# Two output projections run token tile 0 two units ahead, and the normalizations behind them start on tile 0 while the projection is still running

## The chip, the cores and the metric

The kernel runs on one core of one Trainium2 chip. The metric is the device time of one execution in microseconds (us), the median over several runs. The engines are called TensorE (PE, matmuls; its weight loads are PEld), VectorE (DVE), ScalarE (ACT), GpSimd (POOL) and SyncE (SP, which issues most transfers).

## The reference, cut to what matters

The program is two model blocks in a row on 1024 tokens of width 1024. The second block has an even and an odd layer; the even layer also carries 256 context tokens. What the change touches is the end of the even layer, the begin of the odd one and the very end:

```python
# even layer, tokens x and context xc alike
x_new = x + gt * _even_mix(_pre(x, e_norm[i], sh, sc), *args)      # ends in concat(y_a, y_b) @ w_out
xc = xc + gt_c * _even_mix(_pre(xc, e_norm[i], sh_c, sc_c), *args)
# odd layer
cb, cc, cx, cg, q, k, v, ag = _odd_proj(_pre(x, o_norm[i], sh, sc), o_w_in[i])
att = _window_attention(_apply_rope(q, cos, sin), _apply_rope(k, cos, sin), v, k_c, v_c, o_sink[i])
x_new = x + gt * _odd_out(cb, cc, cx, cg, att, ag, o_c_conv_w[i], o_w_out[i])
# end
return _rmsnorm(x, final_norm)
# _pre(x, g, shift, scale) = _rmsnorm(x, g) * (1 + scale) + shift
```

## The kernel before, in words

Activations lie transposed: 128 features on the partitions, 8 chunks of features, tokens along the free dimension. Tokens are cut into tile 0 (tokens 0 to 511), tile 1 (512 to 1023) and, where the context takes part, tile 2 (256 columns); `TILES2` is all three, `TILES1` the first two. A weight *unit* is 128 output features by 1024 input features. A *job* is one unit on one tile: 8 steps k, one for each chunk of input features, and each step is three matmuls (`mm3`: high x high, low x high, high x low), so that float32 accuracy comes out of a faster number format. Every weight and every activation is therefore split into a high part (a cast on ScalarE, `split_hi`, L163) and a low part (a subtraction on VectorE, `split_lo`, L168). Three units fit in the weight buffers, and `units_begun` lets SyncE load the unit after next.

The order on each engine is written out by hand, stage after stage; engines meet at counting semaphores. The stages concerned, in order:

- `eout`: the even output projection, 8 units x 3 tiles, unit by unit (`linear`). After each job VectorE adds the gated product to the residual (L2264), ScalarE squares the result (L230), VectorE adds the square to a running sum (L235). The last job is (unit 7, tile 2).
- `norm5`: the root mean square norm in front of the odd layer. For each tile: 4 small matmuls against the constant `inv_d` (each two instructions, `pe_cols`, L397) give the mean of squares in columns; ScalarE takes the root (L358), VectorE the reciprocal (L439) and four diagonal tiles (L442); a matmul with `ones` (two instructions, `pe_spread`, L402) spreads the factor over a bank. Then for each of 8 chunks VectorE makes the normed value (L466), ScalarE shifts it and writes the high part (L386, L389), and the low part is made on VectorE (even chunks, L427) or on GpSimd (odd chunks, L429). In the kernel before all of this stands behind the last job of `eout`.
- `oin`: the odd input projection. Its first two units, k and v, run as a pair (`first_pair`): tile 0 of both interleaved, then k on tiles 1 and 2, the rest of v. Units for q and the gate follow. A unit's raw weights are loaded once `norm5` is ready.
- `win`: windowed attention, with the convolution branch filled into it; it ends with four products `ycH`, `ycL` (L2500, L2543).
- `oout`: the odd output projection, 8 units x 2 tiles, unit by unit. It reads `ycH/ycL` for steps 0 to 3 and the attention output `qH/qL` for steps 4 to 7. Residual (L2615), square, sum as in `eout`; ScalarE also multiplies by the final gain in place (L2629).
- `norm6`: the final norm: both tiles' `pe_cols`, roots, `pe_spread`, a copy of the factor (L362), and 16 multiplications of 128x512 by that factor, 11 on VectorE (L457) and 5 on GpSimd (L416). SyncE stores each chunk as it gets ready (L2599).

Two helpers that the kernel has already and uses elsewhere: `run_jobs` takes a list of jobs (unit, tile), runs a few of them interleaved at first (`paired`, each `trail` steps behind the one before), calls `between(pe, j, k)` ahead of step k of job j, and waits for a bank where `need(j)` says so. `lagged(units, tiles)` makes such a list in which tile 0 of a unit stands ahead of the other tiles of the unit before:

```python
def lagged(units, tiles, begin=1):
    jobs = [(v, 0) for v in range(begin)]
    for v in range(begin, units):
        jobs += [(v, 0)] + [(v - begin, ti) for ti in range(1, tiles)]
    return jobs + [(v, ti) for v in range(units - begin, units) for ti in range(1, tiles)]
```

Of the kernel before, what the change touches and what calls it, by code (L numbers as in the profile page):

```python
# [24 lines left out]
ALU = mybir.AluOpType  # L25
# [5 lines left out]
P = 128  # L31
D = 1024
KC = D // P
# [66 lines left out]
def build(nc, t):  # L100
# [13 lines left out]
    with es:  # L114
# [123 lines left out]
        class Norm:  # L238
# [36 lines left out]
            def pool_low(self, j):  # L275

                return bool(self.outs) and j % 2 == 1 or self.scaled and j % 3 == 2
# [1482 lines left out]
        def mod_norm(name, layer, tmp, x_ready, squares=None):  # L1760
            return Norm(name, lambda c, ti: tile_of(x, c, ti), TILES2,
                        lambda c, ti: gmod[:, layer, c, vec(ti):vec(ti) + 1],
                        lambda c, ti: modv[:, 24 * layer + c, vec(ti):vec(ti) + 1],
                        lambda part, c, ti: tile_of(u2L if part else u2H, c, ti), tmp, sum_banks=(6, 7, 5), x_ready=x_ready,
                        squares=squares, sum_order=None if squares else [2, 0, 1])


# [466 lines left out]
        eout_squares = Squares("eout_squares", TILES2, A_B)  # L2234
# [5 lines left out]

        def eout_act(act):
            def square(i, s):
                for ti, (c0, n) in enumerate(TILES2):
                    j = (2 * i + s) * T3 + ti
                    act.wait_ge(eout_drained, j + 1 + 2 * T3)
                    f = bass.ds(2 * i + s, 1)
                    src = (hx[:, f, c0:c0 + n] if ti < 2 else x[1][:, f, :]).rearrange("p a n -> p (a n)")
                    eout_squares.act(act, j, (s * T3 + ti) % 2, src, n)

            for v in range(8):  # L2250
                square(v // 2, v % 2)
                split_hi(act, W0["eout"] + v + 2)

        def eout_dve(dve):
            eout_squares.start(dve)
            dve.wait_ge(landed, 80 + 32)
            for i in range(0, 4):
                for s in range(2):
                    for ti, (c0, n) in enumerate(TILES2):
                        dve.wait_ge(eout_done, (2 * i + s) * T3 + ti + 1)  # L2260
                        f = bass.ds(2 * i + s, 1)
# [559 lines left out]
```

## Time and profile before

| what | value |
|---|---|
| time, median of 3 runs | 2137.5 us (2136.45 to 2140.7) |
| profiled execution: time, span of its instructions | 2136.24 us, 2134.4 us |
| TensorE busy, mean granted clock | 96% of the span, 0.985 of full speed |
| VectorE, ScalarE, GpSimd busy | 61%, 36%, 11% |
| TensorE from the last matmul of `eout` to the end of the k and v units | 1567.8 to 1610.7 us |
| `oout` from its first matmul to its last | 2021.0 to 2109.8 us |
| from the last matmul of `oout` to the end | 24.5 us |

The span runs from the first to the last instruction; the time has launch and end around it. Times in the text are counted from the start of the span. The granted clock is a share of 2.4 GHz; it has two levels, 1.0 (2.4 GHz) and 0.5 (1.2 GHz). A busy share says little about what a stage is worth: what counts is which wait ends last in it.

### The profile page before, as it was taken

The page shows a single profiled execution, that of the slowest core. Times are in us where ns is not written, and L with a number is a line of the kernel's source. Part 1 is how long each engine was busy: PE and PEld are TensorE (multiplying, and loading weights), DVE is VectorE, ACT ScalarE, POOL GpSimd, SP SyncE. Part 2 cuts the span into 40 slices and gives each one's busy share as a digit, 9 for nine tenths or more (in the row PEclk, how much of TensorE's full clock was granted, in tenths as well). Part 3 has the DMA queues.
Part 4 walks back from the last instruction along what each step waited for, and adds up shares of the span by engine and source line. Part 5 has one row for each costly group of instructions (what it writes and reads, how often), then busy time and mean ns, then how long its engine had stood idle before and what let it go on. Part 6 is the DMA issues. An engine that isn't in the chain of part 4 may idle for free. (4 is left out here: it accounts for less than half of the span.)

```text
span 2134.4 us, 25901 instructions
## 1 busy us (share of the span) xinstructions
PE 2046.6 (96%) x10182; PEld 1685.3 (79%) x10182; DVE 1298.7 (61%) x2236; ACT 768.7 (36%) x1433; POOL 238.1 (11%) x211
## 2 busy tenths in 40 slices
PE   6999999999999999999999999989999999999796
PEld 4877887888888888887788888778877877888685
DVE  7378867742652562464589896774363356776634
ACT  4256544311310220223441242642152335555432
POOL 2032313000000000002310010000020012222101
PEclk9999999999999999999999999999999999999997
DMA  3102001411321321331231056133122211111212
GB/s 135 60 21 99 31 22 64 162 59 54 131 75 48 109 109 50 109 109 40 65 124 37 34 142 161 67 111 151 40 93 69 79 45 38 38 38 37 105 49 79
DMA packets 47736, 164.75 MB, mean 77 GB/s; under 512 B 5632, under 2 KB 10368, under 8 KB 46464
## 3 DMA queue, kind: packets, MB, share of 16 engines
q1 hardware_dynamic: 43584, 147.02, 20.1%
q0 software_dynamic: 1584, 7.29, 1.7%
q10 hardware_dynamic: 2448, 8.79, 1.1%
q8 instruction: 81, 1.33, 0.2%
q14 instruction: 39, 0.32, 0.1%
HBM read 135.86 MB, written 19.93 MB: 73 GB/s over the span
## 5 line engine op out<-in xcount | busy, mean ns | idle before, releaser
L173 PE MATMUL banks<-u2H,wH 128*128 128x512 f32 (+1 forms) x912 | 347.7, 381 | 11.2 <-POOL u2L L429 6.1
L174 PE MATMUL banks<-u2L,wH 128*128 128x512 f32 (+1 forms) x912 | 338.8, 371 | 0.0
L175 PE MATMUL banks<-u2H,wL 128*128 128x512 f32 (+1 forms) x912 | 338.5, 371 | 0.0
L163 ACT CAST wH<-raw 128x1024 fp32r<-128x1024 f32 x153 | 160.0, 1047 | 288.4 <-DMA raw<-in_wstream 286.4
L173 PE MATMUL banks<-aH,wH 128*128 128x512 f32 x640 | 252.3, 394 | 1.9 <-DVE wL L168 1.7
L175 PE MATMUL banks<-aH,wL 128*128 128x512 f32 x640 | 249.3, 389 | 0.0
L174 PE MATMUL banks<-aL,wH 128*128 128x512 f32 x640 | 249.2, 389 | 0.0
L168 DVE TENSOR_TENSOR wL<-raw,wH 128x1024 fp32r<-128x1024 f32 x153 | 189.4, 1239 | 85.6 <-ACT wH L163 85.2
L173 PEld LDWEIGHTS banks<-u2H,wH 128*128 128x128 f32 x912 | 173.1, 190 | 46.3 <-issue 11.3
L173 PE MATMUL banks<-mH,wH 128*128 128x512 f32 x512 | 200.6, 392 | 2.1 <-DVE wL L168 1.1
L175 PE MATMUL banks<-mH,wL 128*128 128x512 f32 x512 | 199.9, 391 | 0.0
L174 PE MATMUL banks<-mL,wH 128*128 128x512 f32 x512 | 199.9, 390 | 0.0
L175 PEld LDWEIGHTS banks<-u2H,wL 128*128 128x128 f32 x912 | 172.8, 189 | 30.0
L174 PEld LDWEIGHTS banks<-u2L,wH 128*128 128x128 f32 x912 | 173.2, 190 | 28.6 <-issue 1.4
L1942 DVE SCALAR_TENSOR_TENSOR conv_out<-conv_in,par,conv_out 128x1295 f32<-128x1295 f32 x108 | 162.7, 1565 | 0.6
L1100 POOL TENSOR_SCALAR logits<-logits,stat 128x256 f32<-128x256 f32 (+3 forms) x96 | 121.4, 1278 | 340.7 <-DVE stat L975 340.7
L173 PEld LDWEIGHTS banks<-aH,wH 128*128 128x128 f32 x640 | 120.2, 188 | 27.7 <-DVE wL L168 2.2
L175 PEld LDWEIGHTS banks<-aH,wL 128*128 128x128 f32 x640 | 120.2, 188 | 25.1
L174 PEld LDWEIGHTS banks<-aL,wH 128*128 128x128 f32 x640 | 120.3, 188 | 24.5 <-issue 0.5
L1649 DVE TENSOR_TENSOR hm<-banks,hm 128x512 f32<-128x512 f32 x48 | 32.9, 691 | 173.5 <-PE banks L175 173.5
L1508 ACT ACTIVATE relu<-banks 128x512 f32<-128x512 f32 x64 | 38.2, 598 | 244.3 <-PE banks L175 244.3
L1613 DVE SCALAR_TENSOR_TENSOR mod_junk<-mod_w,cvec 128x1024 bf16<-128x1024 f32 x96 | 117.5, 1224 | 5.0
(311 smaller groups left out, 3693.4 us busy)
## 6 DMA issues: line engine op xcount, KB each, us to landing
raw<-in_wstream SPq DMA_DIRECT2D x153, 512.0 KB, 3.5
mod_w<-in_mod_w SPq DMA_DIRECT2D x48, 512.0 KB, 5.2
side_sum<-side_tap POOLq DMA_DIRECT2D x11, 647.5 KB, 5.8
gt<-gates_scratch SPq DMA_DIRECT2D x8, 640.0 KB, 3.9
h<-in_x SPq DMA_DIRECT2D x4, 1024.0 KB, 10.8
hm<-in_x SPq DMA_DIRECT2D x1, 4096.0 KB, 12.3
x_scratch<-x_out SPq DMA_DIRECT2D x2, 2048.0 KB, 7.4
hx<-x_scratch SPq DMA_DIRECT2D x1, 4096.0 KB, 12.2
```

The lines of the kernel that those rows point to most:

```text
L163: act.copy(wH[:, u % R, :], raw[:, u % R, :]).then_inc(weights_hi, 1)
L168: eng.tensor_tensor(wL[:, u % R, :], raw[:, u % R, :], wH[:, u % R, :].bitcast(F32), ALU.subtract)\
L173: first = pe.matmul(out, aH, bH, start=start, stop=False)
L174: pe.matmul(out, aH, bL, start=False, stop=False)
L175: return first, pe.matmul(out, aL, bH, start=False, stop=stop)
L1100: m = pool.tensor_scalar(src, src, stat[:, SUM, k % 3, hs:hs + 1], None, ALU.mult)
L1508: act.activation(relu[:, j % 2, :], bank(j % 4), ACT.Relu).then_inc(up_drained, 1)
L1613: dve.scalar_tensor_tensor(mod_junk[:], mod_w[:, m, :], 1.0, cvec[:, v, :], ALU.mult, ALU.mult, accum_out=modv[:, n, v:v + 1]).then_inc(mo ...
L1649: dve.tensor_tensor(dst, bank(4 + s * 2 + ti), dst, ALU.add).then_inc(down_drained, 1)
L1942: dve.scalar_tensor_tensor(dst, src, w, dst, ALU.mult, ALU.add).then_inc(conv_step, 1)
```

## The change: what it does

1. `eout` goes through a list in which tile 0 of unit v runs ahead of tiles 1 and 2 of unit v-1. The last tile-0 job is thus number 19 of 0 to 23, and four jobs, (6,1), (6,2), (7,1), (7,2), follow it. Into them the norm of tile 0 is put: `pe_cols` ahead of step 4 and `pe_spread` ahead of step 7 of job 20 on TensorE, and root, values, high and low parts of 8 chunks written out in order between the remaining residuals, squares and sums on ScalarE, VectorE and GpSimd. The first two splits of `oin`'s weights stand in the same order. A square root of a constant ahead of the square of job 19 has ScalarE load the table early.
2. Since `y` is still read then, tile 0 of the normed activations gets another place (`w2H`, `w2L`), q moves to where it was, and so do the buffers of the squares and of the values and, in `oout`, `xo`.
3. `oin`'s k and v run as (0,0) and (1,0), interleaved with the second two steps behind, then (0,1), (1,1), (0,2), (1,2). `pe_cols` of tiles 1 and 2 stand ahead of steps 2 and 3 of the first job, `pe_spread` ahead of steps 5 and 6. ScalarE and VectorE take the norm of tiles 1 and 2 there, and take k and v out of the banks in the new order.
4. `oout` runs its list in the same lagged order. Steps 4 to 7 (attention) of jobs (0,0) and (1,0) stand first and wait for the attention of tile 0 only; then steps 0 to 3 of both, which wait for `ycL`. The norm of tile 0 stands in jobs 14 and 15; its 8 final multiplications stand between the residuals of jobs 14 and 15. GpSimd has no part in the final norm any more, VectorE makes all 16 multiplications. Here too a square root of a constant loads the table early.

The core of the diff:

```diff
+        EOUT = [(0, 0)] + [job for v in range(1, 8) for job in ((v, 0), (v - 1, 1), (v - 1, 2))] + [(7, 1), (7, 2)]
+        def eout_split(j):
+            return {0: 2, 4: 3, 7: 4, 10: 5, 13: 6, 16: 7}.get(j)
         def eout_act(act):
+            for j in range(19):
+                eout_square(act, j)
+                if eout_split(j):
+                    split_hi(act, W0["eout"] + eout_split(j))
+            act.activation(rms_cols[:, 2, 0:1], eps[:, 0:1], ACT.Sqrt)
+            eout_square(act, 19)
+            split_hi(act, W0["oin"])
+            norm5.act_root(act, 0)
+            eout_square(act, 20)
+            norm5.act_high(act, 0)
+            norm5.act_high(act, 1)
+            eout_square(act, 21)
+            for c in range(2, 5):
+                norm5.act_high(act, c)
+            split_hi(act, W0["oin"] + 1)
+            norm5.act_high(act, 5)
+            eout_square(act, 22)
+            norm5.act_high(act, 6)
+            norm5.act_high(act, 7)
+            eout_square(act, 23)
         def eout_dve(dve):
+            for j in range(20):
+                eout_residual(dve, j)
+                eout_add(dve, j)
+                if eout_split(j):
+                    split_lo(dve, W0["eout"] + eout_split(j))
+            split_lo(dve, W0["oin"])
+            norm5.dve_root(dve, 0)
+            eout_residual(dve, 20)
+            eout_add(dve, 20)
+            norm5.dve_value(dve, 0)
+            norm5.dve_value(dve, 1)
+            norm5.dve_low(dve, 0)
+            eout_residual(dve, 21)
+            eout_add(dve, 21)
+            norm5.dve_value(dve, 2)
+            norm5.dve_value(dve, 3)
+            norm5.dve_low(dve, 2)
+            norm5.dve_value(dve, 4)
+            norm5.dve_value(dve, 5)
+            norm5.dve_low(dve, 4)
+            split_lo(dve, W0["oin"] + 1)
+            eout_residual(dve, 22)
+            norm5.dve_value(dve, 6)
+            eout_add(dve, 22)
+            norm5.dve_value(dve, 7)
+            norm5.dve_low(dve, 6)
+            eout_residual(dve, 23)
+            eout_add(dve, 23)
         def eout_pe(pe):
-            linear(pe, W0["eout"], 8, TILES2, hl2(yH, yL), eout_done, eout_drained)
+            def between(pe, j, k):
+                if (j, k) == (20, 4):
+                    norm5.pe_cols(pe, 0, 20)
+                if (j, k) == (20, 7):
+                    norm5.pe_spread(pe, 0)
+            run_jobs(pe, W0["eout"], EOUT, TILES2, hl2(yH, yL), lambda j: EOUT[j][0] % 2 * T3 + EOUT[j][1], eout_done, eout_drained,
+                     None, 0, between, need=eout_need)
+        w2H = [sb("w2H0", [KC, TN], A_B, F32R), *u2H[1:]]
+        w2L = [sb("w2L0", [KC, TN], A_B + 16 * KB, F32R), *u2L[1:]]
+        OIN_KV = [(0, 0), (1, 0), (0, 1), (1, 1), (0, 2), (1, 2)]
         def oin_pe(pe):
-            norm5.pe(pe)
-            first_pair(pe, O0, TILES2, hl2(u2H, u2L), lambda s, ti: s * T3 + ti, S["kv_done"], norm5)
+            def between(pe, j, k):
+                if (j, k) in ((0, 2), (0, 3)):
+                    norm5.pe_cols(pe, k - 1, 24)
+                if (j, k) in ((0, 5), (0, 6)):
+                    norm5.pe_spread(pe, k - 4)
+            run_jobs(pe, O0, OIN_KV, TILES2, hl2(w2H, w2L), lambda j: OIN_KV[j][0] * T3 + OIN_KV[j][1], S["kv_done"], S["k_drained"],
+                     norm5, 2, between, need=lambda j: 0, trail=2)
...
+        OOUT = lagged(8, 2)
+        def oout_split(j):
+            return {0: 2, 3: 3, 5: 4, 7: 5, 9: 6, 11: 7}.get(j)
+        def oout_scale(dve, ti):
+            norm6.wait(dve, "rstd_ready", ti + 1)
+            dve.wait_ge(xo_scaled, 14 + 2 * ti)
+            for c in range(KC):
+                dve.tensor_tensor(norm6.x(c, ti), norm6.x(c, ti), norm6.rs[:, ti, :], ALU.mult).then_inc(norm_sems["ready"], 1)
-        def oout_pool(pool):
-            pool.wait_ge(xo_scaled, 2 * KC)
-            norm6.pool(pool)
         def oout_dve(dve):
+            for j in range(14):
+                residual(j)
+                if oout_split(j):
+                    split_lo(dve, W0["oout"] + oout_split(j))
+            norm6.dve_root(dve, 0)
+            residual(14)
+            oout_scale(dve, 0)
+            residual(15)
+            norm6.dve_root(dve, 1)
+            oout_scale(dve, 1)
         def oout_act(act):
+            for j in range(13):
+                square(j)
+                gain(j)
+                if oout_split(j):
+                    split_hi(act, W0["oout"] + oout_split(j))
+            act.activation(rms_cols[:, 2, 0:1], eps[:, 0:1], ACT.Sqrt)
+            square(13)
+            gain(13)
+            norm6.act_root(act, 0)
+            factor(0)
+            for j in (14, 15):
+                square(j)
+                gain(j)
+            norm6.act_root(act, 1)
+            factor(1)
         def oout_pe(pe):
-            pe.wait_ge(S["yc_lo"], HALF)
-            pe.wait_ge(win_o_lo, 2 * NB)
+            blocks = [(0, OQ, False), (1, OQ, False), (0, OY, True), (1, OY, True)] + [(j, OQ + OY, True) for j in range(2, 16)]
+            pe.wait_ge(S["cg_drained"], 2 * HALF)
+            pe.wait_ge(win_o_lo, NB)
+            for n, (j, ks, ends) in enumerate(blocks):
+                if n == 2:
+                    pe.wait_ge(S["yc_lo"], HALF)
+                if n == 4:
+                    pe.wait_ge(win_o_lo, 2 * NB)
+                for i, k in enumerate(ks):
+                    if (j, i) == (14, 4):
+                        norm6.pe_cols(pe, 0, 14)
+                    if (j, i) == (15, 0):
+                        norm6.pe_spread(pe, 0)
...
+            norm6.pe_cols(pe, 1, 16)
+            norm6.pe_spread(pe, 1)
```

## Rows read from the trace of the kernel before

**Rows 1.** Chain that ended last, its end: start us, length us, what.

```profile
2109.87 0.76 DVE xo L2615
...
2112.07 2.74 PE banks L397 x16
2114.81 2.00 PE banks L402 x2
```

**Rows 2.** Timeline of TensorE, end of `eout` to q: start, length, [idle before].

```profile
1567.53 0.28 PE L175 MATMUL banks<-yHc,wL 128*128 128x256 f32 x1
1569.29 3.54 PE L397 MATMUL banks<-inv_d,eout_squares_acc 128*128 128x1 f32 x20 [1.49 <-DVE eout_squares_acc L235]
...
1577.22 0.47 PE L173 MATMUL banks<-u2H,wH 128*128 128x512 f32 x1
...
1613.41 0.50 PE L173 MATMUL banks<-u2H,wH 128*128 128x512 f32 x1 [2.67 <-DVE wL L168]
```

**Rows 3.** Timeline of TensorE, end of `win` and first jobs of `oout`.

```profile
2013.11 0.28 PE L894 MATMUL banks<-pT2L,vz2L 128*128 128x256 f32 x1
2020.99 0.77 PE L173 MATMUL banks<-ycH,wH 128*128 128x512 f32 x1 [7.60 <-PEq L195]
...
2028.07 0.39 PE L173 MATMUL banks<-ycH,wH 128*128 128x512 f32 x1
```

**Rows 4.** Timeline of TensorE at 34 us: a norm inside a running stream.

```profile
34.85 1.05 PE L339 MATMUL banks<-inv_d,x_squares_acc 128*128 128x1 f32 x8 [0.52 <-DVE x_squares_acc L235]
35.77 0.48 PE L173 MATMUL banks<-uH,wH 128*128 128x512 f32 x1
...
37.38 1.13 PE L346 MATMUL banks<-norm_sq,ones 128*128 128x512 f32 x2
```

**Rows 5.** Groups by line, 1456 to 1570 us: busy us, mean ns | idle before.

```profile
L2264 DVE SCALAR_TENSOR_TENSOR hx<-banks,modv,hx 128x512 f32<-128x512 f32 x16 | 12.0, 750 | 48.1 <-PE banks L175 36.4 <-DMA xc<-in_ctx 11.7
L235 DVE TENSOR_TENSOR eout_squares_acc<-eout_squares_acc,eout_squares_sq 128x512 f32<-128x512 f32 x16 | 11.1, 692 | 11.2 <-ACT eout_squares_sq L230 11.2
L230 ACT ACTIVATE eout_squares_sq<-hx 128x512 f32<-128x512 f32 x16 | 10.1, 634 | 77.2 <-DVE hx L2264 77.2
L168 DVE TENSOR_TENSOR wL<-raw,wH 128x1024 fp32r<-128x1024 f32 x8 | 9.8, 1226 | 4.1 <-ACT wH L163 4.1
```

**Rows 6.** Groups by line, 1574 to 1601 us, the chunks of `norm5`.

```profile
L466 DVE SCALAR_TENSOR_TENSOR norm_v<-hx,gmod,banks 128x512 f32<-128x512 f32 x16 | 11.2, 737 | 0.8 <-PE banks L402 0.8
L429 POOL TENSOR_TENSOR u2L<-norm_v,u2H 128x512 fp32r<-128x512 f32 x8 | 10.4, 1296 | 272.2 <-ACT u2H L389 272.2
...
L427 DVE SCALAR_TENSOR_TENSOR u2L<-norm_v,modv,u2H 128x512 fp32r<-128x512 f32 x8 | 7.0, 878 | 1.1
```

**Rows 7.** Line L235 over the run: duration ns min/median/max, first and last start.

```profile
L235 DVE TENSOR_TENSOR x_squares_acc<-x_squares_acc,x_squares_sq x16: 676/692/1604, 7.5 to 33.2; 128x512 f32<-128x512 f32 x16
```

**Rows 8.** Windows: us, busy of PE, PEld, DVE, ACT, POOL; clock; DMA.

```profile
1570.00:1573.00 3.00, 3.00 (x17) 3.00 (x17) 2.85 (x11) 1.67 (x4) 0.00 (x0) 0.55 1.20 513
...
2008.00:2011.00 3.00, 2.12 (x16) 1.91 (x16) 3.00 (x4) 1.35 (x4) 0.00 (x0) 1.00 0.83 360
...
2021.00:2024.00 3.00, 3.00 (x7) 2.42 (x8) 1.30 (x1) 0.00 (x0) 0.00 (x0) 0.50 0.27 83
```

**Rows 9.** Timeline of ScalarE at the begin of the kernel.

```profile
3.28 1.28 ACT L623 ACT_TABLE_LOAD   x1 [3.28 <-issue]
```

**Rows 10.** Page, part 6: transfers, KB each, median us to landing.

```profile
raw<-in_wstream SPq DMA_DIRECT2D x153, 512.0 KB, 3.5
```

**Rows 11.** Timeline of VectorE in the final norm.

```profile
2119.74 3.41 DVE L457 TENSOR_TENSOR xo<-xo,norm_rs 128x512 f32<-128x512 f32 x2
...
2126.40 1.88 DVE L457 TENSOR_TENSOR xo<-xo,norm_rs 128x512 f32<-128x512 f32 x3
...
2128.81 0.68 DVE L457 TENSOR_TENSOR xo<-xo,norm_rs 128x512 f32<-128x512 f32 x1
```

**Rows 12.** Timeline of the SP queue: the last store.

```profile
2131.05 0.61 SPq L2599 DMA_DIRECT2D out_y<-xo  x1
```

More of the change, by code:

```diff
@@ L2239, in eout_sp, with eout_square @@
             loads(sp, "eout", "eout")
-        def eout_act(act):
[L2242 to L2252, printed above, removed]
+        def eout_square(act, j):
+            act.wait_ge(eout_drained, j + 1)
+            eout_squares.act(act, j, j % 2, eout_x(j), TILES2[EOUT[j][1]][1])
@@ L2338, in oin_act @@
         def oin_act(act):
-            norm5.act(act)
+            norm5.act_root(act, 1)
+            norm5.act_root(act, 2)
+            for j in range(KC, 3 * KC):
+                norm5.act_high(act, j)
             norm5.wait_ready(act, 3 * KC)
@@ L2387, in oin_dve @@
             dve.memset(zeros[:], 0.0)
-            norm5.dve(dve)
+            for ti in (1, 2):
+                norm5.dve_root(dve, ti)
+            for j in range(KC, 3 * KC):
+                norm5.dve_value(dve, j)
+                if j > KC:
+                    norm5.dve_low(dve, j - 1)
+            norm5.dve_low(dve, 3 * KC - 1)
             dve.wait_ge(S["rope_loaded"], 32)
@@ L2637, in oout_pe, with residual @@
-        def oout_pe(pe):
-            pe.wait_ge(S["yc_lo"], HALF)
-            pe.wait_ge(win_o_lo, 2 * NB)
-            linear(pe, W0["oout"], 8, TILES1,
-                   lambda part, k, c0, n: ((ycL if part else ycH)[:, k, c0:c0 + n] if k < HALF else
-                                           (qL if part else qH)[:, k - HALF, c0:c0 + n]), oout_done, oout_drained)
-            norm6.pe(pe)
+            def residual(j):
+                dve.wait_ge(oout_done, j + 1)
+                dve.scalar_tensor_tensor(oout_x(j), bank(oout_bank(j)), modv[:, 40 + OOUT[j][0], 0:1], oout_x(j), ALU.mult, ALU.add)\
+                    .then_inc(oout_drained, 1)
+                oout_squares.dve(dve, j, j % 2, OOUT[j][1], TN)
@@ new lines, in oout_dve, with square, gain, factor @@
+            for j in range(14):
[8 more added lines that the diff above has]
+            oout_scale(dve, 1)
+        def oout_act(act):
+            def square(j):
+                act.wait_ge(oout_drained, j + 1)
+                oout_squares.act(act, j, j % 2, oout_x(j), TN)
+            def gain(j):
+                act.activation(oout_x(j), oout_x(j), ACT.Copy, scale=pcol("final_norm2", OOUT[j][0])).then_inc(xo_scaled, 1)
+            def factor(ti):
+                norm6.wait(act, "spread", ti + 1)
+                act.copy(norm6.rs[:, ti, :], bank(norm6.sum_banks[ti])).then_inc(norm_sems["rstd_ready"], 1)
+            for j in range(13):
[13 more added lines that the diff above has]
+            factor(1)
```

113 lines of the change are left out of this document (58 added, 55 removed).

## The prediction, made before the change was run

> **What bounds the kernel now.** I read the chain that ended last first. It runs through TensorE almost everywhere, so only time in which TensorE waits, or works at half clock, can be won, plus what follows its last job. The end of the chain shows the second: job 15 of `oout` is over when its residual starts at 2109.87, and then come residual, square, sum, small matmuls, spread, copy and multiplications one after the other, with TensorE at the slow end of its speed (16 instructions of L397 in 2.74 us, 2.00 us for one spread) [rows 1]. The span ends at 2134.4, 24.5 us after the last job.
>
> The timeline of TensorE shows the first. `eout` ends at 1567.8 (1567.53 + 0.28); the k and v units end at 1613.41 - 2.67 = 1610.7 [rows 2]. That is 42.9 us for work of 2 units. An ordinary 512-column job takes (2109.87 - 2028.07) / 15 = 5.45 us [rows 1, 3], 0.68 a step; a 256-column job I put at 2.9, a little over half. Two units are 2 x (5.45 + 5.45 + 2.9) = 27.6 us, so 15.3 us there are norm and waits: small matmuls and spreads fill 1569.3 to 1577.2, at clock 0.55 in the window shown [rows 2, 8]. The third place is the begin of `oout`: TensorE is idle for 7.60 us, from 2013.4 to 2020.99, and then works at clock 0.50 [rows 3, 8]: the first job takes 7.08 us instead of 5.45, 1.63 lost.
>
> **Part 1: the norm of tile 0 inside `eout`, k and v on tile 0 first.** Call t the end of job 19, the last on tile 0. Jobs 20 to 23 hold 5.45 + 2.9 + 5.45 + 2.9 = 16.7 us, so in the kernel before `eout` ends at t + 16.7 and k and v at t + 59.6.
>
> In the new kernel: residual 0.75, square 0.63, sum 0.69 [rows 5] end at t + 2.2; `pe_cols` stands at step 4 of job 20, t + 2.7, and doesn't wait. In a running stream eight of these instructions push the next matmul back by 0.92 us (35.77 - 34.85), a spread takes 1.13 [rows 4]. Root, reciprocal and diagonals have three steps, 2.0 us, until the spread; the whole norm of three tiles took 7.9 us [rows 2], 2.6 a tile, so at worst 0.6 is missing; I take 0. `eout` thus ends 2.05 later, at t + 18.7, and tile 0's factor is there at t + 6.8.
>
> VectorE sets the rest. Its list makes it wait for job 20 (t + 7.5) ahead of the first value; residual, square, sum bring it to t + 9.7. Then without a break, by [rows 5, 6], the 256-column forms at 0.6 of the others: 8 values (5.9), 4 low parts (3.5), one weight split (1.2), residuals and sums of jobs 21 to 23 (1.65 and 1.5): 13.8 us, so the last sum ends at t + 23.5 with no wait for ScalarE. I add 0.8 for ScalarE, whose squares and high parts stand between, and 0.5 for GpSimd: a sum that meets GpSimd took up to 1.604 instead of 0.692 [rows 7], three sums at most 2.7. That gives t + 24.8.
>
> TensorE has done two steps of k by t + 20.0 and stands at `pe_cols` of tile 1 until t + 24.8: a new stall of 4.8 us, behind which everything of `oin` is queued. Then 0.92 + two steps + 0.5 + four steps, and the spread of tile 1: t + 31.5. Tile 1's chunks follow at 2 x 0.74 + 0.88 a pair [rows 6], 9.4 for four pairs, and 1.7 for the last high part and GpSimd's low part (1.30): t + 42.6. TensorE, done with the tile-0 pair at t + 37.5, ends (0,1) at t + 43.4 and has 5.45 + 2.9 + 2.9 left: t + 54.7. So 4.9 us are won at full clock. What was 42.9 us from `eout`'s end becomes 36.0, but `eout` ends 2.0 later.
>
> The clock takes some back. A stall of 7.60 us was followed by 1.63 lost; the three `pe_cols` of before ran at half clock, 3.54 us for 20 instructions [rows 2] against 2.3 at the price of [rows 4]. I take both here: 1.63, and 0.75 for two of the three tiles, 2.4 in all, so **2.5 us won**; the bounds are 4.9 (the clock holds) and 0 (GpSimd's 2.2 us more on top). The window at 2008 speaks for the first: TensorE was idle for 0.88 of 3.00 us and the clock stayed 1.00; the one at 1570, behind an idle time of only 1.49, speaks for the second [rows 2, 8].
>
> The Trainium skill (TensorE: Matmul & The Clock Gate, Why this matters for your kernels) says that a long idle gap between bursts of matmuls in mid-kernel puts the engine back to half its rate. By that rule the new stall is paid for and the sum stays at 2.5; by the window at 2008 alone it would be 4.9.
>
> The stall of 2.67 us behind v [rows 2] stays: the last copy of v and the two splits of q's first weights still follow the last job. Those weights are loaded when the norm is ready, at about t + 48, some 6.7 us before they are wanted, and a unit lands in 3.5 [rows 10]; the rope table goes ahead of it in the same queue. Every us past that cover would cost one.
>
> At nothing I put: the lagged order in `eout` (unit 2 is wanted after four jobs and not six, but its split hangs on job 0's residual; later units have three jobs between load and use, 13.8 us against 3.5 for the transfer [rows 10] and about 4 for residual, square and both splits, the cast estimated at twice a square for its 1024 columns [rows 5]); the early loads of ScalarE's table (1.28 us [rows 9], while it waits for a job of 5.45; if not covered, or reloaded by the squares, 1.3 each); the moved buffers; the spill of `hx`, issued behind the last residual as before, with nothing waiting for it soon.
>
> **Part 2: `oout`.** The first two blocks are 8 steps, 5.45 us, and start at 2013.4, where TensorE was idle; they end at 2018.85. The wait for `ycL` ends as before, near 2020.9. Ahead of the end of job 13 there are then 14 x 5.45 - 5.45 = 70.8 us: 2091.7, or 2091.5 with the first matmul's own latency out. Before, the second but last job ended its predecessor at 2109.85 - 10.9 = 2098.95: 7.4 won, 5.45 by the early blocks, the rest by the clock, which I let hold over a gap of 2 us; lower bound 5.8.
>
> Behind job 13: 5.45 + 0.92 + 1.13 + 5.45 = 12.95 to the end of job 15. VectorE waits in the sum of job 14 for ScalarE, which is held by the copy of the factor (spread at 7.5; copy, like a square, to 8.2; square): 9.4. Its 8 multiplications: four starts lie 2.41 apart without GpSimd (2126.40 to 2128.81), 0.60 each, against 3.41 for a pair beside GpSimd [rows 11]. They end at 14.2, so residual 15 starts 1.3 late; sum at 16.3. TensorE has been idle for 3.4 us, and I take the prices of [rows 1]: half of 2.74, root and diagonals 1.5, spread 2.00, copy 0.63: the first product is ready at 23.0, the last near 27.2. From the stores: seven issues of 0.61 and the 3.35 us from the last issue (2131.05) to the end [rows 12] give 30.6. From the products: the last one of before ended at 2129.49 [rows 11], 4.9 us ahead of the end, which gives 32.1. Between them I take 31.4. Before, the same stretch was 2134.4 - 2098.95 = 35.45. **4.0 won**; at full clock 5.8. The end is 2091.5 + 31.4 = 2122.9, **11.5 won** in this part, bounds 8 and 13.3.
>
> **The sum.** 2.5 + 11.5 = 14.0 us off the profiled execution's 2136.24: 2122.2. The median of the runs lies 1.26 above that execution, so I forecast 2123.5 for the median.
>
> **The rivals.**
> *A. VectorE and GpSimd get in each other's way in the norm.* For it: the maximum of [rows 7]; against it: the median there is 0.692 and the low parts, 0.878 in the mean, hold the meetings already. Three sums and a split at 0.9 more are 3.1 beyond my 0.5: the sum of job 23 at about t + 27.9, part 1 at -0.6, time 2126.6. From t + 27.3 on the part wins nothing. The Trainium skill (GPSIMD Engine Reference, Key points) says that GpSimd shares its SBUF interfaces with VectorE and contends with instructions that read two SBUF inputs, which the sums and splits do; [rows 11] agree, 3.41 us for two products beside GpSimd against 1.88 for three alone, and by that rule it is this time that comes out.
> *B. The clock holds* at the stall in `oin` and at the end: 4.9 + 13.3 = 18.2, time 2119.3. For it the window at 2008 [rows 8], against it the other two.
> *C. Late weights in the last projection make it slower.* Unit v + 3 is loaded when tile 1 of unit v has ended and split behind the job that starts then: residual 0.75, square 0.63, gain and cast some 1.9 (three times a square, an estimate), split 1.23 [rows 5], 4.5 of the 5.45 us that the next job gives. A load that lands more than 8.5 us after its issue holds TensorE up in each of five units; 2.8 us in each, from a landing of 11.3, eat up all 14.0, and at 12 us the time is 2141. Against it: 3.5 us in the median of 153 [rows 10].
> *D. The change does not do what it says:* the splits and hand-written lists only move the waits, and all that is won is the 5.45 of the early blocks: 2132. For it the 13.8 us of VectorE's unbroken work; against it that TensorE's own waits, 15.3 and 7.6 us, lie at the very places.
>
> **Chances and range.** Forecast 0.5, A 0.24, B 0.2, C 0.02, D 0.04. From B's time less a little to A's with the bounds of part 2 (8 - 0.6: 2130.1) I give 2118 to 2129. A measurement of this kernel tells 0.2%, 4.3 us, from no change. Faster by more 0.95, within 0.03, slower 0.02.
>
> **What would show it.** The new profile should show: `eout` ending 2 us later, and in job 20 no wait at L397 or L402; a stall of about 4.8 us at L397 behind two steps of k, ended by VectorE's sum, and clock 0.5 behind it; k and v ending some 2 to 3 us earlier; the 2.67 us ahead of q unchanged; `oout`'s first matmul at 2013 on this scale, a gap of 2 us, no wait for weights; 12 to 13 us from job 13 to 15, 18 from there to the end. I am wrong if VectorE's sum of job 23 is much later than t + 25, if q's weights come late, or if weights are waited for in the lagged order.

## The result, and the profile after

The changed kernel takes 2126.0 us in the median of four runs, the kernel before 2139.1 beside it: ratio 0.9945 [0.9931, 0.9958], 13 us faster by the medians and 11.8 by the ratio; a second set gave 0.9945 [0.9933, 0.9957]. The profiled execution took 2123.12 us, its span is 2121.3, TensorE is busy for 96% of it at a mean clock of 0.991. The forecast was 2123.5, the range 2118 to 2129. The total came out 2.5 us above the forecast; of the two parts that make it up, the first gave nothing and the second what was forecast or a little more.

Part 1 first. The timeline of TensorE in the changed kernel, from `eout`'s end (1569.51) to q; this answers [rows 2]:

```profile
1570.52 0.39 PE L175 MATMUL banks<-w2H,wL 128*128 128x512 f32 x1
1576.49 1.87 PE L339 MATMUL banks<-inv_d,eout_squares_acc 128*128 128x1 f32 x8 [5.59 <-DVE eout_squares_acc L235]
...
1580.92 0.85 PE L339 MATMUL banks<-inv_d,eout_squares_acc 128*128 128x1 f32 x4
...
1585.57 1.02 PE L346 MATMUL banks<-norm_sq,ones 128*128 128x512 f32 x2
...
1609.67 0.28 PE L175 MATMUL banks<-u2H,wL 128*128 128x256 f32 x1
...
1613.18 0.50 PE L173 MATMUL banks<-w2H,wH 128*128 128x512 f32 x1 [3.23 <-DVE wL L168]
```

After two steps of k TensorE stands for 5.59 us until VectorE's last sum, as foretold, and then works slowly: the eight small matmuls take 1.87 us, against 1.05 for eight such in [rows 4]. The windows of the same kernel show the clock behind the stall (the columns are those of [rows 8]):

```profile
1573.00:1577.00 4.00, 0.51 (x3) 0.51 (x3) 3.01 (x5) 1.66 (x3) 1.26 (x1) 0.59 0.62 262
1577.00:1581.00 4.00, 4.00 (x15) 3.42 (x14) 1.05 (x5) 0.26 (x1) 0.00 (x0) 0.50 0.91 393
1581.00:1585.00 4.00, 4.00 (x15) 3.34 (x14) 0.65 (x3) 0.26 (x1) 0.00 (x0) 0.63 1.03 389
1585.00:1589.00 4.00, 4.00 (x18) 2.96 (x17) 2.24 (x4) 1.56 (x3) 0.00 (x0) 1.00 0.15 57
```

The half clock falls on the very instructions that the next stretch of the norm waits for. Why the sum itself is late is seen in the same kernel's timeline of VectorE, which shows two of its three last sums:

```profile
1563.57 1.31 DVE L235 TENSOR_TENSOR eout_squares_acc<-eout_squares_acc,eout_squares_sq 128x256 f32<-128x256 f32 x1 [0.48 <-ACT eout_squares_sq L230]
...
1575.15 1.28 DVE L235 TENSOR_TENSOR eout_squares_acc<-eout_squares_acc,eout_squares_sq 128x256 f32<-128x256 f32 x1 [0.70 <-ACT eout_squares_sq L230]
```

and in that of GpSimd at the same times:

```profile
1563.31 1.28 POOL L429 TENSOR_TENSOR w2L<-norm_v,w2H 128x512 fp32r<-128x512 f32 x1 [250.67 <-ACT w2H L308]
...
1574.89 1.26 POOL L429 TENSOR_TENSOR w2L<-norm_v,w2H 128x512 fp32r<-128x512 f32 x1 [2.82 <-ACT w2H L308]
```

Each sum of 256 columns begins while a low part of GpSimd runs, and ends 0.29 and 0.28 us behind it; in the kernel before, such a sum took 0.42 to 0.43 us. The Trainium skill (SBUF — State Buffer, SBUF: two separate sides) says that whichever of the two engines starts first holds the shared port pair for its whole instruction when VectorE reads two SBUF inputs; these four rows agree, except that the sums end less than 0.42 us behind GpSimd, so not all of a sum waited.

Part 2: the timeline of TensorE at the begin and at the end of `oout`, which answers [rows 1, 3]:

```profile
2013.53 0.40 PE L173 MATMUL banks<-qH,wH 128*128 128x512 f32 x1
...
2021.07 0.50 PE L173 MATMUL banks<-ycH,wH 128*128 128x512 f32 x1 [1.91 <-DVE ycL L2624]
...
2108.14 1.05 PE L339 MATMUL banks<-inv_d,oout_squares_acc 128*128 128x1 f32 x8 [3.34 <-DVE oout_squares_acc L235]
2110.67 2.07 PE L346 MATMUL banks<-norm_sq,ones 128*128 128x512 f32 x2 [1.48 <-DVE norm_sq L317]
```

and of VectorE at the end, with the last residual and the 8 multiplications of tile 1:

```profile
2105.95 0.74 DVE L2711 SCALAR_TENSOR_TENSOR xo<-banks,modv,xo 128x512 f32<-128x512 f32 x1
...
2113.39 4.90 DVE L2695 TENSOR_TENSOR xo<-xo,norm_rs 128x512 f32<-128x512 f32 x8 [2.78 <-ACT norm_rs L2736]
```

The first blocks start where TensorE idled before, and a wait of 1.91 us is left of 7.60. The last residual starts at 2105.95, the last product ends at 2118.29. From the end of the attention on TensorE (in the changed kernel the start of the first block, 2013.5) to the end of the span it is 2121.3 - 2013.5 = 107.8 us, against 2134.4 - 2013.4 = 121.0: 13.2 won in this execution.

### The profile page after: what moved, and what is told of

Its sections match the earlier page's. It is cut to its first block and busy times, and to the rows that moved or that the text cites. A ratio compares the mean times of both kernels' runs of the same rounds, so it can differ in the third digit from the quotient of the medians.

```text
span 2121.3 us, 25905 instructions
## 1 busy us (share of the span) xinstructions
PE 2038.9 (96%) x10182; PEld 1679.8 (79%) x10182; DVE 1298.2 (61%) x2241; ACT 767.6 (36%) x1435; POOL 229.4 (11%) x206
## 3 DMA queue, kind: packets, MB, share of 16 engines
q0 software_dynamic: 1584, 7.29, 1.8%
## 5 line engine op out<-in xcount | busy, mean ns | idle before, releaser
L173 PE MATMUL banks<-u2H,wH 128*128 128x512 f32 (+1 forms) x704 | 260.0, 369 | 3.9 <-POOL u2L L429 2.1
L174 PE MATMUL banks<-u2L,wH 128*128 128x512 f32 (+1 forms) x704 | 256.3, 364 | 0.0
L175 PE MATMUL banks<-u2H,wL 128*128 128x512 f32 (+1 forms) x704 | 256.3, 364 | 0.0
L173 PEld LDWEIGHTS banks<-u2H,wH 128*128 128x128 f32 x704 | 133.3, 189 | 26.7 <-issue 3.7
L175 PEld LDWEIGHTS banks<-u2H,wL 128*128 128x128 f32 x704 | 133.1, 189 | 21.3
L174 PEld LDWEIGHTS banks<-u2L,wH 128*128 128x128 f32 x704 | 133.4, 190 | 20.1 <-issue 0.2
## 6 DMA issues: line engine op xcount, KB each, us to landing
hm<-in_x SPq DMA_DIRECT2D x1, 4096.0 KB, 13.6
hx<-x_scratch SPq DMA_DIRECT2D x1, 4096.0 KB, 12.1
```

The costliest lines, as they stand in the source:

```text
L173: first = pe.matmul(out, aH, bH, start=start, stop=False)
L174: pe.matmul(out, aH, bL, start=False, stop=False)
L175: return first, pe.matmul(out, aL, bH, start=False, stop=stop)
```

## The experiments

All ratios are to the kernel before, run on the same chip. Distances "behind `eout`" are counted from the end of its last matmul: in the changed kernel the last sum is at 6.9, the end of tile 1's spread at 17.1, the end of k and v at 40.4, the start of q at 43.7; in the kernel before, k and v end at 42.9 and q starts at 45.6, but `eout` is some 1.8 us shorter there. In the twelve profiled executions with the changed `eout` its end lies anywhere from 1569.5 to 1573.7 us, so rows of different executions are compared within a stage and not by their place in the span.

### The parts by themselves

```diff
part1_only: eout_*, oin_* of after; oout_*, norm6 of before
part2_only: eout_*, oin_* of before; oout_*, norm6 of after
```

> The even output projection and the odd input projection of the changed kernel, with the last projection and the final norm of the kernel before. Theory T: the chain from the last sum to the spread of tile 1 ran at half clock and ate what the early norm of tile 0 gained, so k and v end where they did and this part alone is worth 0 to 0.5 us of 2139 (ratio 0.9998, between 0.9995 and 1.0005). The prediction's sum: 2.5 us won, ratio 0.9988. Rival: the part loses by itself (late weights of q, a longer eout) and only looks neutral beside part 2: ratio above 1.001.

> The even output projection and the odd input projection of the kernel before, with the last projection and the final norm of the changed kernel. Theory T: all of the gain is here, 13.4 us from the end of the attention to the end of the span: ratio 0.9937, time about 2126. By the prediction's sizes 11.5 us: 0.9946. Rival: part 1 gives part of it (its buffers or its earlier k and v help later stages): under 10 us, ratio above 0.9953.

Part 1 alone: 2138.5 us, ratio 1.0001 [0.9992, 1.001]. Part 2 alone: 2126.0 us, 0.9944 [0.9931, 0.9956]. The gain is all in part 2, and the prediction's 2.5 us for part 1 (0.9988) lie outside the interval. Part 2's 12.0 us by the ratio agree with 11.5 as well as with 13.2.

### The clock behind the stall

```diff
+                if (j, k) == (0, 2):
+                    for i in range(23):
+                        pe.matmul(bank(3), wH[:, O0 % R, 0:P], w2H[0][:, 0, :], start=True, stop=True)
                 if (j, k) in ((0, 2), (0, 3)):
                     norm5.pe_cols(pe, k - 1, 24)
```

> The changed kernel with 23 additional matmuls of 128x512 (operands that are there already, into a bank that is not in use and is opened anew later) ahead of the small matmuls of tile 1, in the stall of 5.59 us; they compute nothing that is read. Theory T, the clock ate the gain: with TensorE busy the granted clock stays at 1.00 behind the stall, the 8 small instructions take 0.9 us instead of 1.87, the spread of tile 1 ends 6.7 us behind the last sum instead of 10.2, and k and v end 3.4 us earlier: time 3.4 us under the changed kernel, ratio to the kernel before 0.9929. Rival 1, the clock falls whatever TensorE does there: no difference, 0.9945. Rival 2, the later waits (chunks of tile 1, weights of q) take it back: spread 3.4 us earlier, but q starts less than 1 us earlier, ratio 0.994 to 0.9945.

Ratio 0.9926 [0.9914, 0.9939], 4 us under the changed kernel; the two intervals overlap, so the rows have to carry the reading. TensorE's timeline of this kernel, with the stall filled:

```profile
1578.38 1.05 PE L339 MATMUL banks<-inv_d,eout_squares_acc 128*128 128x1 f32 x8 [0.42 <-DVE eout_squares_acc L235]
...
1583.94 1.02 PE L346 MATMUL banks<-norm_sq,ones 128*128 128x512 f32 x2
```

and its windows:

```profile
1577.00:1581.00 4.00, 3.58 (x22) 2.82 (x21) 2.63 (x7) 0.27 (x1) 1.04 (x1) 1.00 1.23 524
1581.00:1585.00 4.00, 4.00 (x18) 3.02 (x18) 0.66 (x4) 0.26 (x1) 0.00 (x0) 1.00 0.91 393
```

The sum comes at the same distance (7.0), but the spread ends at 13.6 instead of 17.1 and k and v at 37.0 instead of 40.4: 3.4 us, as theory T had it, and q starts 4.0 us earlier, so that rival 2 falls. Work that computes nothing pays here, because the clock stays at 1.00 for the chain behind it.

### The place of the wait

```diff
-                if (j, k) in ((0, 2), (0, 3)):
-                    norm5.pe_cols(pe, k - 1, 24)
-                if (j, k) in ((0, 5), (0, 6)):
+                if (j, k) in ((0, 6), (1, 4)):
+                    norm5.pe_cols(pe, 1 + j, 24)
+                if (j, k) in ((1, 5), (1, 6)):
                     norm5.pe_spread(pe, k - 4)
```

> The changed kernel with the small matmuls of tiles 1 and 2 moved back in the pair on tile 0: ahead of steps (0,6) and (1,4), the spreads ahead of (1,5) and (1,6). Ten steps of tile 0 (6.8 us) then stand where TensorE idled for 5.59 us. Theory T, the place of the wait cost the stall and the clock: no stall over 0.5 us, clock 1.00, spread of tile 1 done some 11.4 us after eout's end instead of 17.2, last chunk of tile 1 about 22.6 us after it instead of 28.3, k and v end 5 to 6 us earlier; q waits for its weights some 3.5 us as before: time 5 to 6 us under the changed kernel, ratio 0.992. Rival, the chunks of tile 1 on VectorE, ScalarE and GpSimd (11 us) are the bound from the last sum on, wherever TensorE waits, and the moved spread makes them begin later still: the stall moves to (0,1), and the gain is under 1.5 us, ratio 0.994 or more.

Ratio 0.9915 [0.9901, 0.993], 2121.3 us. TensorE's timeline:

```profile
1580.72 1.05 PE L339 MATMUL banks<-inv_d,eout_squares_acc 128*128 128x1 f32 x8 [0.19 <-DVE eout_squares_acc L235]
...
1589.64 0.47 PE L173 MATMUL banks<-u2H,wH 128*128 128x512 f32 x1 [1.01 <-POOL u2L L429]
```

The stall is 0.19 us, the spread ends at 11.6 (11.4 expected), k and v at 34.9, 5.5 us earlier than in the changed kernel. What is left are waits for chunks of tile 1, 3.0 us in all, of which the second row shows the first. Theory T holds: the small matmuls stood too early in TensorE's list, and real work covers the sum.

### The sums that meet GpSimd

```diff
                     elif self.pool_low(j):
+                        if self.v_at == 6 * KB and j in (1, 7):
+                            pool.wait_ge(squares_added, self.squares.added0 + self.squares.FREE + (22 if j == 1 else 24))
                         self.low(pool, j, norm_sems["ready_pool"])
```

> The changed kernel with GpSimd's low parts of chunks 1 and 7 of tile 0 held back until VectorE has made the sums of jobs 21 and 23. Theory T, the two sums took 1.3 us instead of 0.43 because GpSimd's low parts ran beside them: both take 0.43 now, the last sum ends 5.2 us behind the end of eout instead of 7.0, the stall is 3.9 us instead of 5.6, and k and v end 1.7 us earlier: ratio 0.9937. Rival, what comes behind the sums takes it back, or the sums are long for another reason (256 columns behind ScalarE's square): last sum within 0.5 us of the changed kernel, ratio 0.9943 to 0.9945.

Ratio 0.9934 [0.9922, 0.9947]. The sums in VectorE's timeline:

```profile
1564.42 0.43 DVE L235 TENSOR_TENSOR eout_squares_acc<-eout_squares_acc,eout_squares_sq 128x256 f32<-128x256 f32 x1 [0.48 <-ACT eout_squares_sq L230]
...
1575.13 0.42 DVE L235 TENSOR_TENSOR eout_squares_acc<-eout_squares_acc,eout_squares_sq 128x256 f32<-128x256 f32 x1 [0.70 <-ACT eout_squares_sq L230]
```

and TensorE behind them:

```profile
1575.61 1.05 PE L339 MATMUL banks<-inv_d,eout_squares_acc 128*128 128x1 f32 x8 [3.85 <-DVE eout_squares_acc L235]
...
1579.01 0.85 PE L339 MATMUL banks<-inv_d,eout_squares_acc 128*128 128x1 f32 x4
...
1582.76 1.02 PE L346 MATMUL banks<-norm_sq,ones 128*128 128x512 f32 x2
```

Both take their plain time, the last ends at 5.2 and the stall is 3.85 us, as expected. k and v end at 36.8, 3.6 us earlier and not 1.7: behind the shorter stall the small matmuls took 1.05 us and the spread ended 8.2 us behind the sum instead of 10.2, so this execution also lost less to the clock, which fell later: the four small matmuls of tile 2 still took 0.85 us, in `late_cols` and `warm` 0.50. By time alone it can't be told from the changed kernel; the rows show the collision.

### The weights of q

```diff
 oin_sp:
+            load_unit(sp, O0 + 2)
             norm5.wait_ready(sp, 3 * KC)
...
 oin_act, oin_dve: behind the last act_high and dve_low
+            split_hi(act, O0 + 2)
+            split_lo(dve, O0 + 2)
...
 (the same load and splits go from their later places)
```

> The changed kernel with the first weight unit of q loaded as soon as k has begun, ahead of the wait for the norm in SyncE's list, and split behind the last chunk of the norm instead of behind the copies of v. Theory T, what TensorE waits for ahead of q are these weights (loaded late, split behind the copies): the wait of 3.23 us falls to 0.7 to 1.0, and with it the half clock behind it (1.75 us) goes in part: 2.3 to 4 us under the changed kernel, ratio 0.993. Rival, TensorE waits for the next thing, the rotation of k with the rope table or the copies out of the banks: gain under 1 us, 0.9941 to 0.9945.

Ratio 0.9925 [0.9912, 0.9939], 2121.2 us. TensorE's timeline of this version ahead of q:

```profile
1610.51 0.47 PE L173 MATMUL banks<-w2H,wH 128*128 128x512 f32 x1 [0.71 <-PEq L2392]
```

A window behind it in this version:

```profile
1614.00:1619.00 5.00, 5.00 (x23) 4.13 (x22) 0.00 (x0) 0.00 (x0) 0.00 (x0) 1.00 0.01 2
```

and in the changed kernel:

```profile
1614.00:1619.00 5.00, 5.00 (x16) 3.94 (x15) 0.35 (x1) 0.00 (x0) 0.00 (x0) 0.66 0.36 105
```

The wait falls from 3.23 to 0.71 us, and the clock no longer falls behind it (from 1610.5 to 1615.5, right behind the wait, it is 1.00 as well): 2.5 us, and 0.34 x 5 = 1.7 more. Load and splits were moved together; which of the two counts more isn't shown. A wait of 2.67 us stood here in the kernel before too [rows 2], with the clock at 0.66 in the same window; neither kernel needs it.

### The early blocks of the last projection

```diff
-            blocks = [(0, OQ, False), (1, OQ, False), (0, OY, True), (1, OY, True)] + ...
+            blocks = [(0, OQ, False), (0, OY, True), (1, OQ, False), (1, OY, True)] + ...
-                if n == 2:
+                if n == 0:
                     pe.wait_ge(S["yc_lo"], HALF)
```

> The changed kernel, but the last projection waits for the last low product ahead of its first matmul and takes the two halves of jobs 0 and 1 one after the other. Theory T, the early blocks gain their own length and the clock: TensorE idles some 7.4 us again, the granted clock falls to 0.50 behind it, and 5.45 + 1.6 = 7 us are lost: 7 us over the changed kernel, ratio to the kernel before 0.9978. Rival 1, the clock holds over the gap: 5.45 lost, 0.997. Rival 2, the wait ends later when the early blocks run, since they were in something's way: under 4 us lost, ratio under 0.9963.

2132.8 us, ratio 0.9969 [0.9959, 0.998]: 5 us more than the changed kernel by the ratio, 6.8 by the medians. TensorE's timeline of this version:

```profile
2010.77 0.42 PE L892 MATMUL banks<-pT2H,vz2H 128*128 128x256 f32 x1 [3.24 <-DVE pT2L L955]
...
2012.49 1.91 PE L876 MATMUL banks<-ident,logits 128*128 128x128 f32 x8
...
2024.09 0.77 PE L173 MATMUL banks<-qH,wH 128*128 128x512 f32 x1 [7.56 <-DVE ycL L2624]
```

and its windows:

```profile
2020.00:2024.00 4.00, 0.00 (x0) 0.00 (x0) 3.65 (x3) 2.05 (x3) 0.48 (x1) 0.50 0.00 0
2024.00:2027.00 3.00, 2.91 (x7) 2.36 (x8) 1.34 (x1) 0.00 (x0) 0.00 (x0) 0.50 0.31 68
```

From the end of the attention (2016.54) to the end of the span (2131.6) it is 115.1 us against 107.8: 7.3, theory T's 5.45 for the blocks and the rest from the half clock. Against the repeat below (110.1), which loses some time to the clock itself, it is 5.0. The times alone leave room for rival 1; the clock in the windows doesn't. So the blocks are worth 5 to 7 of the 12 us; the rest of part 2, the norm of tile 0 inside the last jobs and VectorE alone at the products, was not taken apart by a run.

### The same kernel again, and the tail

> The changed kernel once more, as a base for the others: ratio to the kernel before 0.9945, within 0.9935 to 0.9955, by every theory.

```diff
+            for i in range(20):
+                if i == 14:
+                    norm6.pe_cols(pe, 1, 16)
+                pe.matmul(bank(2), wH[:, u % R, 0:P], qH[:, 0, 0:TN], start=True, stop=True)
             norm6.pe_spread(pe, 1)
```

> The changed kernel with 14 matmuls of 128x512 more ahead of the small matmuls of tile 1 in the final norm and 6 more ahead of its spread, where TensorE idles 3.34 and 1.48 us; they go into an unused bank and nothing reads them. Theory T, half clock at the end is only a small term: the spread takes 1.0 us instead of 2.07, the end comes 1.1 us earlier, ratio 0.994, hardly to be told from the changed kernel by time, but plain in the rows. By the prediction, which put 1.8 us of the tail to the clock, 1.8 us: 0.9937. Rival, the last product doesn't set the end, the stores do: spread shorter, end the same.

The repeat gave 0.9945 [0.9933, 0.9957], the tail with the additional matmuls 0.994 [0.9928, 0.9952], by time alone the same. TensorE's timeline of the repeat:

```profile
2021.87 0.72 PE L173 MATMUL banks<-ycH,wH 128*128 128x512 f32 x1 [1.91 <-DVE ycL L2624]
2022.38 0.63 PE L174 MATMUL banks<-ycL,wH 128*128 128x512 f32 x1
...
2110.54 1.73 PE L339 MATMUL banks<-inv_d,oout_squares_acc 128*128 128x1 f32 x8 [3.35 <-DVE oout_squares_acc L235]
2113.74 2.08 PE L346 MATMUL banks<-norm_sq,ones 128*128 128x512 f32 x2 [1.47 <-DVE norm_sq L317]
```

and of the kernel with the filled tail:

```profile
2112.84 1.05 PE L339 MATMUL banks<-inv_d,oout_squares_acc 128*128 128x1 f32 x8 [0.18 <-DVE oout_squares_acc L235]
2115.38 1.12 PE L346 MATMUL banks<-norm_sq,ones 128*128 128x512 f32 x2
```

From the last residual to the end of the span the filled tail takes 14.5 us (2110.65 to 2125.1), the changed kernel 15.4 and its repeat 16.0: the clock at the end is worth 0.9 to 1.6 us, and the end of the span moves with the products. The rival falls in the rows.

### All of it together

```diff
best, on early_q:
+                if (j, k) == (1, 1): norm5.pe_cols(pe, 1, 23)
+                if (j, k) == (1, 3): norm5.pe_spread(pe, 1)
+                if (j, k) == (0, 6): norm5.pe_cols(pe, 2, 24)
+                if (j, k) == (1, 5): norm5.pe_spread(pe, 2)
...
+  the root of tile 2 (act_root, dve_root) between the first chunks of tile 1
pairs, on best with low_after_sum:
-  trail=2)
+  trail=2, pairs=2)     # (0,1) and (1,1) interleaved as well
+  pe_cols 1 at (1,2), pe_spread 1 at (1,4), pe_cols 2 at (1,5), pe_spread 2 at job 2, step 3
pairs_k_first, on pairs with tail_warm, in oin_dve:
-            dve.wait_ge(S["rope_loaded"], 32)
             norm5.wait_ready(dve, 3 * KC)
             dve.wait_ge(S["kc_hi"], 1)
             dve.tensor_tensor(k2L[:, SEQ:TOK], ...)
+            dve.wait_ge(S["rope_loaded"], 32)
```

> All that should help in the first part, on top of the changed kernel: the small matmuls of tile 1 ahead of step (1,1) and waiting only for the sum of tile 1's last job, its spread ahead of (1,3), those of tile 2 ahead of (0,6) and (1,5), the root of tile 2 between the first chunks of tile 1, and the early load and split of q's first weights. Theory T, the bound is the chain from tile 1's last sum over the chunks: spread of tile 1 some 8.4 us behind eout's end instead of 17.2, its last chunk near 19.5 instead of 28.2, k and v end some 7 us earlier, the wait ahead of q about 1 us: 9 to 11 us under the changed kernel, ratio 0.9895. Rival, the chunks of tile 2 or VectorE's list, which is unbroken from eout on, are the next bound: k and v end 4 us earlier as with the late small matmuls alone, 6 to 7 us under the changed kernel, ratio 0.9915.

> The version best with three edits more: k and v on tile 1 interleaved like on tile 0, so that two steps of TensorE stand for each chunk; the small matmuls and the spread of tile 1 two steps later, those of tile 2 ahead of (1,5) of tile 0 and of the fourth step of tile 1; and GpSimd's low parts behind the sums as in low_after_sum. Theory T, on tile 1 TensorE waited for chunks that come 1.4 us apart and are used up in 0.68: with the pair it waits no more, clock 1.00 from eout to q, k and v end 31 to 32 us behind the end of eout (best 35.8, the changed kernel 40.4, 30.6 without any wait), 4 us under best: about 2114.5 where the kernel before takes 2139, ratio 0.9887. Rival, VectorE's unbroken list is the bound, and the waits move to tile 2: under 1.5 us less than best, ratio 0.9898 or more.

> The version pairs with the low part of k's context columns made ahead of VectorE's wait for the rope table, and with the additional matmuls of tail_warm at the end. In pairs TensorE waited 2.85 us ahead of q for a bank that VectorE emptied late, since it stood behind the wait for the rope table. Theory T: this wait falls to 0.7 us as in best and early_q, the clock then holds, and the tail gives 1.1 us: 3 to 4.5 us under pairs, ratio 0.9882. Rival: the rope table stays the bound one step later (the rotation of k ahead of q's second unit): only the tail's 1.1 us, ratio 0.9895 or more.

`best`: 2118.5 us, 0.9905 [0.9892, 0.9919], between theory and rival. The spread of tile 1 ended at 9.4 (8.4 expected), k and v at 35.8 (33.4 or so expected). TensorE's timeline shows where it was lost: both spreads waited for diagonals in VectorE's list, that of tile 2, put too early, for 2.18 us; the clock was 0.68 in the window from 1585 to 1589.

```profile
1578.68 1.12 PE L346 MATMUL banks<-norm_sq,ones 128*128 128x512 f32 x2 [1.03 <-DVE norm_sq L317]
...
1585.22 0.70 PE L346 MATMUL banks<-norm_sq,ones 128*128 128x256 f32 x2 [2.18 <-DVE norm_sq L317]
```

`pairs`: 2116.9 us, 0.9901 [0.9888, 0.9914]. k and v end at 30.4 without one wait, a little better than expected, but the time is only 1.7 us under `best` and not 4: a new wait of 2.85 us stands ahead of q. The timeline of `pairs`, VectorE and TensorE:

```profile
1602.23 0.42 DVE L2500 TENSOR_TENSOR k2L<-banks,k2H 128x256 fp32r<-128x256 f32 x1 [4.35 <-DMA rope<-in_rope]
...
1602.96 0.47 PE L173 MATMUL banks<-w2H,wH 128*128 128x512 f32 x1 [2.85 <-PEq L2398]
```

and that of `pairs_k_first`, TensorE:

```profile
1602.96 0.47 PE L173 MATMUL banks<-w2H,wH 128*128 128x512 f32 x1 [0.71 <-PEq L2398]
```

VectorE emptied a bank of k only behind its wait for the rope table, and TensorE waited for the bank. With the wait for the rope table moved behind that line, TensorE's wait is 0.71 us. `pairs_k_first` takes 2111.9 us, 0.9876 [0.9859, 0.9892]: 27 us under the kernel before, 14 under the changed one. It is 5 us under `pairs`, a little more than expected: 2.1 from the wait, 1.7 from the clock behind it (1.00 instead of 0.66 from 1603 to 1608) and some 1.1 from the tail, though the two intervals just overlap.

## Why the prediction was right, and where it was not

*What bounds the kernel, and the places to win.* Right. In part 2 the stalls named there are the ones that went; in part 1 a new one took the place of the old. Each edit that took away an idle time of TensorE, or the half clock behind it, moved the rows of its stage by what it took away.

*Part 1, up to the last sum.* Job 19 ends at 1551.05, so t + 18.5 is `eout`'s end (18.7 predicted), L339 and L346 inside job 20 don't wait, and the last sum is at t + 25.4 (24.8). The 0.6 too late hide errors both ways: GpSimd was priced at 0.5 and cost 2 x 0.87 = 1.7 in the two sums; ScalarE was priced at 0.8, and the same two sums waited 0.48 and 0.70 for its squares; against these 1.6 us too few, VectorE's own work was priced about a us too high. What was put at nothing in `eout` stayed nothing: behind its first matmul TensorE waits for no weights, and ScalarE's table load (1546.57 to 1547.85) is over before the next square is due at 1551.87.

*The clock behind the stall.* The step that failed most, by size. It was priced with the loss of another stall, 1.63, and 0.75 for two `pe_cols`, 2.4 in all. From sum to end of spread it was 10.2 us instead of 6.7, so 3.5 were lost; in the five other executions with the same stall it was 9.4 to 10.0, 2.7 to 3.3 lost. `warm` gave 3.4 back by keeping the clock up, and nothing else was changed there. The price fell short because the matmuls stayed at 0.63 us until 1584, 7.5 us long, where [rows 3] have 1.63 lost behind 7.60 us of idle time, some 3.3 us at half clock. Most of the loss, about 2.6 us, fell on the six ordinary steps in that stretch; the small matmuls lost 1.0 and the spread, at 1.02 us, nothing. Why the half clock lasted longer here isn't shown.

*The chunks of tile 1.* Right: 11.1 us from the spread to the last low part, as summed, and then 12.3 to the end of k and v (12.1).

*The stall ahead of q.* Said to stay at 2.67, with 6.7 us of cover for the load. The cover was 6.4 us, but the load landed 6.9 us after its issue, behind the rope table in the same queue; the copy to the high part waited 0.46 us, and the stall became 3.23. The changed kernel's SP queue and ScalarE:

```profile
1603.55 0.33 SPq L2365 DMA_DIRECT2D rope<-in_rope  x1
1603.92 10.12 SPq L152 DMA_DIRECT2D raw<-in_wstream  x3
```

```profile
1610.82 1.04 ACT L163 CAST wH<-raw 128x1024 fp32r<-128x1024 f32 x1 [0.46 <-DMA raw<-in_wstream]
```

The prediction took the median landing of all loads, 3.5 us, and named the rope table without giving it a price.

Together 0.6 for the late sum, 1.1 for the clock, 0.2 behind the chunks and 0.6 for q's weights make 2.5 us: all of what part 1 was to win (q starts at t + 62.1, in the kernel before at 59.6 + 2.7 = 62.3). That it wins nothing is shown by `part1_only`; that clock, collision and weights are the causes, by `warm`, `low_after_sum` and `early_q`, each of which brought back its own term in the rows.

*Part 2.* The gap of 2 us (1.91), the full clock over it, and no waits for weights in the lagged order came as written; by job 13 (2092.1) 7.0 us are won of 7.4. The tail from there to the end took 29.2 us, not 31.4: the last residual at 13.9 (14.2), `pe_cols` 1.05 and not 1.37, and the end 3.0 us behind the last product, which the prediction took for 4.2. Another 0.6 is a slip in its sum: 16.3 + 1.37 + 1.5 + 2.00 + 0.63 and a product of 0.60 put the first product at 22.4 and not at 23.0. So 0.4 less was won ahead of job 13 and 2.2 more behind it, 13.2 in the profiled execution. In the repeat the same stretch took 110.1 us, 10.9 won: the clock fell in the gap of 1.91 us and again ahead of the last `pe_cols`. Of nine profiled executions with this projection and tail five took 107.8 and four 108.3 to 110.1. The 12.0 of `part2_only` lies between, so 11.5 was a fair middle of a term that the clock moves by two us; that the tail's surplus and the clock's losses nearly cancel in the median is luck.

*The rivals.* The time lies near that of A, and A's mechanism is real, but with 1.7 us of the 3.6 that its sum gave it; the rest of the miss came from the clock and q's weights, so the agreement in time is chance. The weight split and the 512-column sums didn't meet GpSimd. B didn't come: in all six executions with the stall of 5.6 us in `oin` the eight small matmuls behind it took 1.86 or 1.87 us. Its evidence was stronger than the prediction read it: the idle time at the window of 2008 [rows 8] was 3.25 us long, of which only 0.88 lies inside the window. C and D didn't come; behind the gap of 1.91 us no job of `oout` waited for anything.

## What to carry to other kernels

Where an engine waits inside a list, first ask how much work behind that place doesn't need the result: moving the small matmuls by eight steps brought k and v 5.5 us forward, where the whole early norm of tile 0 had won nothing. The long stalls here cost their length and then the clock of what followed, so price both, and put no such stall ahead of a chain that others wait for. When one wait is gone, read what the next one is for: twice here it was a line that stood behind an unrelated wait in a list written by hand (q's weights behind the norm, a bank behind the rope table).

## What the runs showed of the hardware

The same gap doesn't always have the same price. After 1.91 us of idle time at the same place of the same program the next matmuls took 0.39 us in one execution and 0.63 in the other; a gap of 3.24 us in the attention left the clock at 1.00 in the kernels before and after, and was followed by half clock in `no_early_blocks` and `tail_warm`, whose instructions up to there are those of the changed kernel. Eight transposes behind the gap took 1.91 us in `no_early_blocks` (its timeline above) and 1.04 in the changed kernel:

```profile
2008.98 0.36 PE L892 MATMUL banks<-pT2H,vz2H 128*128 128x256 f32 x1 [3.24 <-DVE pT2L L955]
...
2010.06 1.04 PE L876 MATMUL banks<-ident,logits 128*128 128x128 f32 x8
```

Stalls of 5.6 and 7.6 us were followed by the half clock each time. The Trainium skill (TensorE: Matmul & The Clock Gate, Why this matters for your kernels) says that long idle gaps between bursts put TensorE back to half its rate; the long stalls agree. The short gaps here went either way; behind the end of the attention this comes with 2.3 us of difference between two executions of the changed kernel (107.8 and 110.1).

VectorE beside GpSimd loses only in some instructions: a sum of 256 columns took 1.31 us instead of 0.43, and a low part of 512 columns, which also reads two arrays, up to 1.01 instead of 0.75, while the normed values, which read a bank and one array, kept their 0.70 us each (1.39 and 1.40 for two) beside GpSimd's low parts of tile 1.
